# Scaled probabilities, split convolution scaling, and turned quarters on TensorE in a hybrid decoder layer

## Chip, cores and metric

One core of a Trainium2 chip runs the whole layer in one launch. The metric is device time in microseconds (us) of that launch, the median of several runs. A profiled execution stands beside them.

## What is computed

One layer of a hybrid decoder on 1024 tokens of width 1024, all in float32:

```python
h = rms_norm(x); P = h @ W_in + b_in            # [b_gate | c_gate | u | q | k | v]
conv = b_gate * conv3_causal(c_gate * u)        # 512 channels
p = exp(scores + bias - m)                      # window 128, two key blocks of 128 per query block
attn = (p / (sum(p) + exp(sink - m))) @ v       # 8 q heads, 2 kv heads, width 64
x = x + concat(rms_norm(conv), rms_norm(attn)) @ W_out + b_out
h2 = rms_norm(x); top-4 of 32 experts, gates = softmax of the four logits
y[e] = (min(g, 7) * sigmoid(1.702 * min(g, 7)) * (clip(l, -7, 7) + 1)) @ w2[e] + b2[e]
       # hid = h2 @ w1[e] + b1[e], g = even columns, l = odd columns
out = x + sum over the chosen experts of gate * y[e]
```

## The kernel before

Synchronisation is written by hand: each engine has its own instruction stream, and semaphores (`event`) tie them. The order within an engine is the order of the text. SP issues the weight loads, GpSimd (POOL) the indirect gathers and scatters.

**The mixer** (function `mixer`) goes over 8 blocks of 128 tokens, block 0 and block 7 written out, the others in a loop. In a block TensorE projects the four convolution chunks (`project_conv`, line 839), turns q and k (895), makes the scores (906), then turns the probabilities (`turn_p`, 850): for each half i of four heads and each key block j, four products of a 128x128 square of `probs` with a diagonal matrix `diag`, whose diagonal is 1/denominator, so that the product is the scaled transpose. `attend` (862) multiplies with v; it waits for the pT copies of both halves, of which DVE makes (i,0) (`read_turned`, 668) and ScalarE (i,1) (`turn_read_act`, 513). Then come the convolution part of the output projection (923, two halves of four k), with the sum of the convolution's squares between the halves (869), the first transposes of the next block's rows (804), the attention part (936), the next block's q projection (813), the transposes of h2 (945), k and v (817), the router (829, 954). DVE's order in a block is: gate_input (615), taps (622 to 627), gate_output (634) of the chunks, bias and maximum of the scores (645, 709, 716), `normalise` of each half (660 to 662), the copies (668), sums of squares (729, 737), the rest. GpSimd does the taps of chunks 2 and 3 (`add_taps_pool`, 439 to 445), then scales all of conv_y to conv_s in one instruction (462), the reciprocal roots (429), and adds b_out to the residual (468).

**The join.** The second function, `experts`, starts behind a barrier. DVE splits the gates into three bfloat16 parts (1341 to 1345), makes `token`, `limits` and `marks`, reads each token's rank in its expert from TensorE (1354), and works out a table of jobs, sorted by size (1358 to 1399). From it come the list of the first job's tokens (`match_tokens`, `list_tokens`, `read_list`) and two gathers of their rows on GpSimd (1213). ScalarE copies some counters and clears the banks (1266 to 1271). TensorE turns the biases (1674, 1677), which DVE copies (1444 to 1446). `first_rows` turns the gathered rows (1582, 16 squares; each of four steps needs both gathers), and DVE copies them to xT (1407).

**The jobs.** A job is one expert with up to 256 tokens: here 15 wide jobs (over 128 tokens, lines 1601, 1412 to 1438) and 17 narrow ones (up to 128). Each loads six slots of 2 MB of weights. A slot is loaded again for the next job once TensorE has used it (SP, 1157). In a narrow job (`narrow_job`) the token rows are the stationary side: `first_layer` has 4 parts of 512 columns (1625), `second_layer` 2 outputs of 512 columns over 8 k (1637), in the order m=0 and m=1 over k 0 to 5, then m=0 and m=1 over k 6 and 7. Each part of the first layer goes through DVE (`clip_rows`, `finish_rows`), ScalarE (sigmoid, 1298) and DVE again (`turn_act`, 16 transposes of 32x64, 1138) into act_T, of which part c holds k = 2c and 2c+1. Then DVE turns the next job's gathered rows into xT (`turn_x`, 16 transposes of 32x256, 1138), scales b2 by the gates (1543), and forms the output rows (1548), which GpSimd adds to the output (1257). The gather for the next job (1213) is issued after its list is read, behind part 1. TensorE's next job waits for xT.

Of the kernel before, what the change touches and what calls it, by code (L numbers as in the profile page):

```python
# [23 lines left out]
P = 128  # L24
# [111 lines left out]
def mixer(nc, x_rows, out_rows, h2_rows, rel_rows, norm_mix, w_in, b_in, conv_w, q_norm, k_norm, sinks,  # L136
          rel_bias, out_norm_conv, out_norm_attn, w_out, b_out, norm_ffn, w_router, b_router, const,
          cst, tri_b, ones_b, picked, gates, before):

    ident = cst[:, C_ID:C_ID + P]  # L140
    with ExitStack() as ctx:
# [65 lines left out]
        diag = sb("diag", [P, NH, P])  # L207
# [84 lines left out]
        conv_scaled = event("conv_scaled")  # L292
        conv_summed = event("conv_summed")
# [8 lines left out]
        diag_ready = [event(f"diag_ready_{i}") for i in ("first", "second")]  # L302
# [28 lines left out]
        vstep = Steps(sem("vector_step"), 23)  # L331
# [84 lines left out]
        def _(pool):  # L416
# [30 lines left out]
            def one_block(t, more, first=False):  # L447
# [32 lines left out]
        def _(act):  # L480
# [40 lines left out]
            def one_block(t, more):  # L521
# [13 lines left out]
                exp_half(t, 1)  # L535
                add_u_bias(t, 3)
# [32 lines left out]
        def _(dve):  # L569
# [86 lines left out]
            def normalise(t, i):  # L656
# [36 lines left out]
            nc.vector.tensor_copy(ones_b[:], cst[:, C_ONES:C_ONES + P])  # L693
            def one_block(t, more, first=False):
# [106 lines left out]
        def _(pe):  # L801
# [42 lines left out]
            def turn_p(t, i):  # L844

                wait(pe, diag_ready[i], t)
# [41 lines left out]
            def one_block(t, more):  # L888
# [73 lines left out]
def experts(nc, h2_rows, out_rows, w1, b1, w2, b2, cst, tri_b, ones_b, picked, gates, before):  # L962
# [8 lines left out]
    with ExitStack() as ctx:  # L971
# [338 lines left out]
        def _(dve):  # L1310
# [139 lines left out]
            for i in range(4):  # L1450
                read_xT(0, i)
# [305 lines left out]
```

## Time and profile before

| | |
|---|---|
| median of 3 runs | 2076.33 us (2073.55 to 2079.98) |
| profiled execution | 2082.2 us |
| its span, first to last instruction | 2080.4 us |
| mean granted TensorE clock | 0.979 |
| busy: PE, DVE, ACT, POOL | 1982.3, 1418.9, 352.5, 238.6 us |
| moved by DMA | 504.21 MB, mean 242 GB/s |

Engines: PE is TensorE's matmuls, PEld its weight loads, which overlap them, DVE VectorE, ACT ScalarE, POOL GpSimd, SP SyncE. A row of the timeline has its start, its length (of one instruction, or of a group of neighbours with their count), the engine, the line and what it writes and reads; the bracket tells idle time ahead of it and what ended it. A float32 matmul shows as two instructions (passes), a transpose by the identity as one. A PE instruction's length reaches past the start of the next, since matmuls are pipelined.

### The profile page before, as it was taken

The numbers are of one execution on the slowest core, as the hardware profiler recorded it, in microseconds if no ns is written. First come the engines' busy times: TensorE is split into PE (matmuls) and PEld (weight loads), VectorE is DVE, ScalarE is ACT, GpSimd is POOL, SyncE is SP. The second block draws the span as 40 slices with busy tenths as digits, with TensorE's granted clock in tenths as the row PEclk, the third lists the DMA queues.
The fourth block names the chain that finished last, engine by engine and source line by source line (L and its number), as shares of the span: only waits on it lengthen the run. The fifth ranks groups of instructions, "written<-read, shape, count | busy, mean of one in ns | idle before, by whom it ended". The sixth has DMA issues, their size and how long they took to land.

```text
span 2080.4 us, 30074 instructions
## 1 busy us (share of the span) xinstructions
PE 1982.3 (95%) x10692; PEld 1453.0 (70%) x10692; DVE 1418.9 (68%) x4145; ACT 352.5 (17%) x732; POOL 238.6 (11%) x305
## 2 busy tenths in 40 slices
PE   7899999994999999989999999999999999999996
PEld 6577777772999999989999999834444444444442
DVE  3345545544276677777876777778887888788876
ACT  2122222221011222212222222210000000000000
POOL 1212222211000111110011111110000000000000
PEclk9999999996899999999999999999999999999998
DMA  9411001002956777767788888999999999999992
GB/s 299 102 41 40 20 30 40 30 31 94 334 169 232 233 259 247 271 211 263 266 283 282 301 294 294 324 332 327 366 356 355 368 367 359 358 362 368 367 353 67
DMA packets 238481, 504.21 MB, mean 242 GB/s; under 512 B 7525, under 2 KB 20881, under 8 KB 236257
## 3 DMA queue, kind: packets, MB, share of 16 engines
q1 hardware_dynamic: 224736, 454.93, 61.1%
q0 software_dynamic: 11392, 40.18, 7.8%
q10 hardware_dynamic: 2304, 8.39, 1.0%
q8 instruction: 38, 0.62, 0.1%
q14 instruction: 11, 0.08, 0.0%
HBM read 475.48 MB, written 28.00 MB: 242 GB/s over the span
## 4 chain that ended last, share of the span: by engine, by line
issue 41%; PE 28%; POOL 2%; DMA 2%; DVE 2%; POOLq 0%; ACT 0%; DVEq 0%
PE ps_unit L1601 28%; DMA out_dram<-y_rows,idx_cur 1%; POOL out_dram L1257 1%; POOL x_got L1213 1%; DMA x_got<-h_rows,idx_next 0%; DVE act_T L1422 0%; DVE sig L1420 0%; DVE glu L1412 0%; ACT sig L1280 0%; PE ps_list L1570 0%; PE ps_unit L1582 0%; POOL carrier L1209 0%; POOL out_dram L1225 0%; POOLq L990 0%; DVE match L1325 0%
## 5 line engine op out<-in xcount | busy, mean ns | idle before, releaser
L1601 PE MATMUL ps_unit<-xT,w_slot 128*128 128x136 f32 (+6 forms) x3840 | 528.3, 300 | 16.3 <-issue 15.3
L1601 PEld LDWEIGHTS ps_unit<-xT,w_slot 128*128 128x128 f32 x3840 | 523.0, 198 | 17.6 <-issue 17.5
L1625 PE MATMUL ps_unit<-w_slot,xT 128*128 128x512 f32 x1088 | 477.2, 597 | 8.1 <-DVE xT L1138 8.1
L1625 PEld LDWEIGHTS ps_unit<-w_slot,xT 128*128 128x128 f32 x1088 | 204.5, 190 | 266.3 <-issue 266.3
L1138 DVE STREAM_TRANSPOSE xT<-x_got 32x256 f32<-32x256 f32 x668 | 291.1, 436 | 16.9 <-DMA x_got<-h_rows,idx_next 7.7
L1601 PE MATMUL ps_unit<-act_T,w_slot 128*128 128x136 f32 (+6 forms) x1920 | 264.0, 299 | 7.0 <-DVE act_T L1422 6.7
L1138 DVE STREAM_TRANSPOSE act_T<-act_rows 32x64 f32<-32x64 f32 x1088 | 256.8, 236 | 16.3
L1601 PEld LDWEIGHTS ps_unit<-act_T,w_slot 128*128 128x128 f32 x1920 | 259.5, 191 | 10.0 <-DVE act_T L1422 5.6
L1637 PE MATMUL ps_unit<-w_slot,act_T 128*128 128x512 f32 x544 | 236.5, 592 | 1.3 <-DVE act_T L1138 1.3
L1438 DVE STREAM_TRANSPOSE y_rows<-yT 32x256 f32<-32x256 f32 x396 | 172.6, 436 | 38.9 <-ACT yT L1287 33.5
L1637 PEld LDWEIGHTS ps_unit<-w_slot,act_T 128*128 128x128 f32 x544 | 103.3, 190 | 131.7 <-issue 129.4
L839 PE MATMUL ps_c<-hT,w_in_sb 128*128 128x128 f32 x1536 | 176.8, 276 | 0.0
L839 PEld LDWEIGHTS ps_c<-hT,w_in_sb 128*128 128x128 f32 x1536 | 173.5, 192 | 3.1 <-issue 3.1
L1209 POOL TENSOR_TENSOR carrier<-carrier 128x1 f32<-128x1 f32 x64 | 15.0, 235 | 1393.0 <-issue 592.5
L1298 ACT ACTIVATE sig<-glu 128x256 f32<-128x256 f32 x68 | 28.3, 416 | 646.1 <-DVE glu L1504 646.1
L1412 DVE TENSOR_SCALAR glu<-ps_unit,b_cur 128x256 f32<-128x256 f32 x120 | 57.5, 480 | 77.5 <-PE ps_unit L1601 76.9
L1420 DVE TENSOR_TENSOR sig<-sig,glu 128x256 f32<-128x256 f32 x120 | 51.0, 425 | 69.6 <-ACT sig L1280 52.6
L1280 ACT ACTIVATE sig<-glu 128x256 f32<-128x256 f32 x120 | 50.0, 417 | 276.7 <-DVE glu L1412 276.5
L1500 DVE TENSOR_TENSOR hid<-ps_unit,b_row 128x512 f32<-128x512 f32 x68 | 47.0, 691 | 72.5 <-PE ps_unit L1625 72.4
L1287 ACT ACTIVATE yT<-ps_unit,b_cur 128x256 f32<-128x256 f32 x120 | 50.4, 471 | 210.2 <-PE ps_unit L1601 210.2
L923 PE MATMUL ps_s<-w_out_sb,conv_s 128*128 128x512 f32 x128 | 61.0, 622 | 6.9 <-DMA w_out_sb<-in_w_out_dram 6.9
L1292 ACT ACTIVATE y_rows<-y_rows,gate_cur 128x1024 f32<-128x1024 f32 x30 | 32.8, 1141 | 179.2 <-DVE y_rows L1438 179.2
(247 smaller groups left out, 1505.9 us busy)
## 6 DMA issues: line engine op xcount, KB each, us to landing
w_slot<-in_w_dram SPq DMA_DIRECT2D x192, 2048.0 KB, 10.4
b_row<-in_b_dram SPq DMA_DIRECT2D x17, 1024.0 KB, 12.1
b_row<-in_b_dram SPq DMA_DIRECT2D x17, 512.0 KB, 13.6
w_in_sb<-in_w_in_dram SPq DMA_DIRECT2D x12, 512.0 KB, 8.5
x_in<-in_x_dram SPq DMA_DIRECT2D x8, 512.0 KB, 3.5
x_res<-in_x_dram SPq DMA_DIRECT2D x8, 512.0 KB, 4.9
out_dram<-x ACTq DMA_DIRECT2D x8, 512.0 KB, 5.1
h_rows<-h ACTq DMA_DIRECT2D x8, 512.0 KB, 3.2
```

The source lines that it names most:

```text
L839: last = pe.matmul(ps_c[:, c % 2, j * P:(j + 1) * P], w_in_sb[:, k, first:first + P], hT[:, k, :], start=(k == 0), stop=(k == KD - 1))
L923: last = pe.matmul(ps_s[:, n * 512:(n + 1) * 512], conv_s[:, k, :], w_out_sb[:, k, n * 512:(n + 1) * 512], start=(k == 0), stop=(k == CC - 1))
L1138: last = nc.vector.transpose(out[c * Q:(c + 1) * Q, :, tokens], rows.rearrange("p (k c j) -> p k c j", c=P // Q, j=Q)[:, :, c, :])
L1280: nc.scalar.activation(sig[:, p % 3, :], glu[:, p % 3, :], ACT.Sigmoid, scale=ALPHA).then_inc(sig_ready[p].sem, 1)
L1287: last = nc.scalar.activation(yT[:, m, :], ps_unit[p % RING][:, u, :], ACT.Identity, bias=b2_cur[:, m:m + 1])
L1412: v.tensor_scalar(glu[:, p % 3, :], ps_unit[p % RING][:, 0, :], b1_cur[:, 2 * p:2 * p + 1], LIMIT, ALU.add, ALU.min).then_inc(glu_ready[p] ...
L1420: v.tensor_tensor(sig[:, p % 3, :], sig[:, p % 3, :], glu[:, p % 3, :], ALU.mult).then_inc(scaled[p].sem, 1)
L1438: last = v.transpose(rows[:, :, c, :], yT[c * Q:(c + 1) * Q, :, a * Q:(a + 1) * Q])
L1500: v.tensor_tensor(hid[:, c % 2, :], ps_hid[c], b1_row[:, c * LW:(c + 1) * LW], ALU.add).then_inc(hid_read[c].sem, 1)
L1601: last = pe.matmul(ps_unit[p % RING][:, u, 0:n], w, moving[:, k, 0:n], start=(k == 0), stop=(k == KD - 1))
L1625: last = pe.matmul(ps_hid[c], xT[:, k, 0:P], w_slot[:, c, k, :], start=(k == 0), stop=(k == KD - 1))
L1637: last = pe.matmul(ps_out[m], act_T[:, k, 0:P], w_slot[:, W1_LOADS + m, k, :], start=(k == 0), stop=(k == KD - 1))
```

## The change

- Probabilities: `diag` and its product are gone. DVE multiplies the first half of `probs` by 1/denominator; the second half is scaled by four ScalarE instructions after its exponentials. TensorE turns `probs` with the identity.
- conv_s is scaled in two instructions on GpSimd: chunks 0 to 2 ahead of the taps of chunk 3, and chunk 3 after them. TensorE waits for the second at k = 3 of the first half.
- `token`, `limits`, `marks` are made by DVE in the mixer, ahead of block 0.
- In the join ScalarE does the three casts of the gates, the reads of the turned biases and two of the four xT copies. DVE's second subtraction moves behind the job fields. `first_rows` turns all first halves after the first gather, then all second halves.
- Narrow jobs: the last part of act_rows (k = 6, 7) is turned by TensorE, two transposes between m=0 and m=1 over k 0 to 5, into a bank of its own, and copied by ScalarE. ScalarE also scales b2.

```diff
 # mixer, GpSimd
-                add_taps_pool(t, 3)
-                for i in range(CC):
+                for i in range(CC - 1):
                     wait(pool, conv_out[i], t)
                 wait(pool, conv_mixed, t - 1)
-                nc.gpsimd.tensor_tensor(conv_s[:], conv_y[:], conv_g_col.unsqueeze(2).broadcast_to([P, CC, P]),
+                nc.gpsimd.tensor_tensor(conv_s[:, 0:3, :], conv_y[:, 0:3, :], conv_g_col[:, 0:3].unsqueeze(2).broadcast_to([P, 3, P]),
                                         ALU.mult).then_inc(conv_scaled.sem, 1)
+                add_taps_pool(t, 3)
+                wait(pool, conv_out[3], t)
+                nc.gpsimd.tensor_tensor(conv_s[:, 3:4, :], conv_y[:, 3:4, :], conv_g_col[:, 3:4].unsqueeze(2).broadcast_to([P, 1, P]),
+                                        ALU.mult).then_inc(conv_scaled_last.sem, 1)
 # mixer, ScalarE
                 exp_half(t, 1)
+                wait(act, denom_ready, t)
+                for s in range(HALF, NH):
+                    last = nc.scalar.activation(probs[:, s, :], probs[:, s, :], ACT.Copy, scale=rdenom[:, s:s + 1])
+                last.then_inc(probs_ready[1].sem, 1)
                 add_u_bias(t, 3)
 # mixer, VectorE, normalise
+                if i == 1:
+                    nc.vector.reciprocal(rdenom[:, part], denom[:, part]).then_inc(denom_ready.sem, 1)
+                    return
                 then_wait(t, nc.vector.reciprocal(rdenom[:, part], denom[:, part]))
-                nc.vector.tensor_tensor(diag[:, part, :], ident.unsqueeze(1).broadcast_to([P, HALF, P]),
-                                        rdenom[:, part].unsqueeze(2).broadcast_to([P, HALF, P]),
-                                        ALU.mult).then_inc(diag_ready[i].sem, 1)
+                nc.vector.tensor_tensor(probs[:, part, :], probs[:, part, :],
+                                        rdenom[:, part].unsqueeze(2).broadcast_to([P, HALF, 2 * P]),
+                                        ALU.mult).then_inc(probs_ready[i].sem, 1)
 # mixer, TensorE
-                        last = pe.matmul(ps_turned[i][j][:, h * P:(h + 1) * P], probs[:, s, j * P:(j + 1) * P], diag[:, s, :],
-                                         start=True, stop=True)
+                        last = pe.transpose(ps_turned[i][j][:, h * P:(h + 1) * P], probs[:, s, j * P:(j + 1) * P], ident)
...
+                        if n == 0 and k == CC - 1:
+                            wait(pe, conv_scaled_last, t)
 # experts, ScalarE
+            nc.scalar.copy(gate_parts[:, :, 0, :], gates[:]).then_inc(parts_cast[0], 1)
...
+            act.wait_ge(biases_turned, 1)
...
+            for i in (0, 2):
+                wait(act, x_turned[i], 0)
+                nc.scalar.copy(xT[:, 2 * i:2 * i + 2, :], ps_x[i][:]).then_inc(xT_read, 1)
...
+                wait(act, last_turned, t)
+                nc.scalar.copy(act_T[:, KD - 2:KD, 0:P], ps_act[:, 0:2, :]).then_inc(actT_ready[W1_LOADS - 1].sem, 1)
+                wait(act, b2_loaded, t)
+                wait(act, cur_ready, q)
+                nc.scalar.activation(b2_row[:], b2_row[:], ACT.Copy, scale=gate_cur[:, 0:1]).then_inc(b2_gated.sem, 1)
 # experts, VectorE, narrow job
-                    turn_act(t, c)
+                    if c < W1_LOADS - 1:
+                        turn_act(t, c)
...
-                wait(dve, b2_loaded, t)
-                v.tensor_scalar(b2_row[:], b2_row[:], gate_cur[:, 0:1], None, ALU.mult).then_inc(b2_gated.sem, 1)
 # experts, TensorE
+            def turn_last(t):
+                wait(pe, rows_ready[W1_LOADS - 1], t)
+                first = (W1_LOADS - 1) % 2 * PW
+                for k in range(2):
+                    last = pe.transpose(ps_act[:, k, :], act_rows[:, first + k * P:first + (k + 1) * P], ident)
+                last.then_inc(last_turned.sem, 1)
...
-                for ks in (range(0, 6), range(6, KD)):
-                    for m in range(2):
-                        second_layer(t, q, m, ks)
+                second_layer(t, q, 0, range(0, KD - 2))
+                turn_last(t)
+                second_layer(t, q, 1, range(0, KD - 2))
+                for m in range(2):
+                    second_layer(t, q, m, range(KD - 2, KD))
...
-                for i in range(4):
-                    turn_x(0, i)
+                for h, gathered in enumerate((gathered_a, gathered_b)):
+                    wait(pe, gathered, 0)
+                    for i in range(4):
+                        turn_x(i, h)
```

## Rows read from the trace of the kernel before

**Rows 1.** Busy time by stretches: us, busy us by engine, PEclk, DMA share, GB/s

```profile
271.00:324.00 53.00, 53.00 (x324) 38.51 (x323) 25.84 (x62) 14.53 (x39) 11.07 (x16) 1.00 0.12 40
1498.00:1540.00 42.00, 41.69 (x105) 18.36 (x104) 34.54 (x119) 2.95 (x5) 3.02 (x4) 1.00 1.01 363
1389.00:1392.50 3.50, 3.50 (x5) 1.32 (x4) 3.19 (x13) 0.00 (x0) 1.68 (x2) 0.53 1.04 392
```

**Rows 2.** Who waited for whom, whole run: us in total, times, longest

```profile
PE ps_unit L1625 <- DVE xT L1138: 8.1, 16, 3.4
...
PE ps_s L923 <- DMA w_out_sb<-in_w_out_dram: 6.9, 1, 6.9
```

**Rows 3.** Timeline of one block of the mixer, TensorE (start us, us, what)

```profile
234.88 1.06 PE L850 MATMUL ps_q<-diag,probs 128*128 128x128 f32 x8
...
238.60 1.94 PE L862 MATMUL ps_c<-pT,v_keys 128*64 128x512 f32 x8
...
262.44 1.04 PE L945 MATMUL ps_s<-cst,h 128*128 128x128 f32 x8
263.31 2.32 PE L817 MATMUL ps_kv<-w_in_sb,hT 128*128 128x256 f32 x10
```

**Rows 4.** The same block, VectorE

```profile
230.67 0.69 DVE L662 TENSOR_TENSOR diag<-cst,small 128x512 f32<-128x512 f32 x1
...
237.76 0.69 DVE L668 COPY pT<-ps_s 128x512 f32<-128x512 f32 x1 [1.09 <-PE ps_s L850]
```

**Rows 5.** The same block, ScalarE

```profile
231.88 0.49 ACT L506 ACTIVATE probs<-probs,small 128x256 f32<-128x256 f32 x1
...
235.08 0.37 ACT L498 ACTIVATE conv_u<-ps_c,vectors 128x128 f32<-128x128 f32 x1 [2.52 <-PE ps_c L839]
```

**Rows 6.** The same block, GpSimd

```profile
231.70 1.11 POOL L439 TENSOR_TENSOR conv_t<-conv_x,vectors 128x128 f32<-128x128 f32 x3 [16.29 <-DVE conv_x L615]
...
238.97 1.04 POOL L462 TENSOR_TENSOR conv_s<-conv_y,vectors 128x512 f32<-128x512 f32 x1 [0.80 <-DVE conv_y L634]
```

**Rows 7.** Timeline of the join between mixer and experts

```profile
496.85 0.17 DVE L1339 SCALAR_TENSOR_TENSOR token<-cst 128x8 f32<-128x8 f32 x1 [1.34 <-PEq L126]
...
499.37 0.42 DVE L1354 COPY rank<-ps_list 128x256 f32<-128x256 f32 x1
...
510.50 0.16 DVE L1332 COPY list_sb<-ps_list 128x10 f32<-128x10 f32 x1
...
523.17 3.65 PE L1582 MATMUL ps_unit<-cst,x_got 128*128 128x128 f32 x16 [12.94 <-DMA x_got<-h_rows,idx_next]
...
527.88 4.45 PE L1601 MATMUL ps_unit<-xT,w_slot 128*128 128x208 f32 x12 [1.06 <-DVE xT L1407]
```

**Rows 8.** The tile x_got from 505 to 530 us: two gathers, issue to landing

```profile
DMA to landing us min/median/max: 7.8/8.8/9.9
```

**Rows 9.** Timeline of the narrow jobs in their steady state

```profile
1460.29 13.90 PE L1637 MATMUL ps_unit<-w_slot,act_T 128*128 128x512 f32 x32
...
1462.98 3.98 DVE L1138 STREAM_TRANSPOSE act_T<-act_rows 32x64 f32<-32x64 f32 x16
...
1466.99 7.18 DVE L1138 STREAM_TRANSPOSE xT<-x_got 32x256 f32<-32x256 f32 x16
...
1474.50 14.00 PE L1625 MATMUL ps_unit<-w_slot,xT 128*128 128x512 f32 x32 [0.31 <-DVE xT L1138]
...
1496.07 1.01 POOL L1213 DMA_INDIRECT x_got<-h_rows,idx_next  x1
...
1516.56 3.69 PE L1625 MATMUL ps_unit<-w_slot,xT 128*128 128x512 f32 x8 [0.31 <-DVE xT L1138]
```

**Rows 10.** DMA issues of the page: count, KB each, median us to landing

```profile
w_slot<-in_w_dram SPq DMA_DIRECT2D x192, 2048.0 KB, 10.4
...
x_got<-h_rows,idx_next POOLq DMA_INDIRECT x49, 7.0
```

**Rows 11.** Timeline, start of the second narrow job

```profile
1388.68 15.69 PE L1625 MATMUL ps_unit<-w_slot,xT 128*128 128x512 f32 x32 [3.41 <-DVE xT L1138]
```

More of the change, by code:

```diff
@@ L137, in mixer @@
           rel_bias, out_norm_conv, out_norm_attn, w_out, b_out, norm_ffn, w_router, b_router, const,
-          cst, tri_b, ones_b, picked, gates, before):
+          cst, tri_b, ones_b, picked, gates, before, token, limits, marks):
     ident = cst[:, C_ID:C_ID + P]
@@ L206, in mixer @@
         pT = sb("pT", [P, 2, 2, HALF * P])
-        diag = sb("diag", [P, NH, P])
         attn_ss = sb("attn_ss", [P, P])
@@ L301, in mixer @@
         exped = [event(f"exped_{i}") for i in ("first", "second")]
-        diag_ready = [event(f"diag_ready_{i}") for i in ("first", "second")]
+        denom_ready = event("denom_ready_second")
+        probs_ready = [event(f"probs_ready_{i}") for i in ("first", "second")]
         p_turned = [[event(f"p_turned_{i}{j}") for j in range(2)] for i in ("first", "second")]
@@ L693, in _ @@
             nc.vector.tensor_copy(ones_b[:], cst[:, C_ONES:C_ONES + P])
+            nc.vector.scalar_tensor_tensor(out=token[:], in0=cst[:, C_TOK:C_TOK + NB], scalar=32.0,
+                                           in1=cst[:, C_TOK + NB:C_TOK + 2 * NB], op0=ALU.mult, op1=ALU.add)
+            nc.vector.tensor_scalar(limits[:, 0, :], cst[:, C_IOTA:C_IOTA + len(SIZES) - 1], float(SIZE_STEP), float(SIZES[0]),
+                                    ALU.mult, ALU.add)
+            nc.vector.tensor_scalar(marks[:], cst[:, C_IOTA:C_IOTA + len(SIZES)], float(P),
+                                    float(P * (2 - len(SIZES))), ALU.mult, ALU.add)
             def one_block(t, more, first=False):
@@ L844, in turn_p @@
             def turn_p(t, i):
-                wait(pe, diag_ready[i], t)
+                wait(pe, probs_ready[i], t)
                 for j in range(2):
@@ L959, in _, with experts @@
             one_block(NB - 1, False)
-def experts(nc, h2_rows, out_rows, w1, b1, w2, b2, cst, tri_b, ones_b, picked, gates, before):
+def experts(nc, h2_rows, out_rows, w1, b1, w2, b2, cst, tri_b, ones_b, picked, gates, before, token, limits, marks):
     ident = cst[:, C_ID:C_ID + P]
@@ L1008, in experts @@
         place_cur = sb("place_cur", [P, NB])
-        token = sb("token", [P, NB])
         match = sb("match", [P, NB, CAP], BF16)
@@ L1049, in experts @@
         ps_list = ps("ps_list", [P, 512])
+        ps_act = ps("ps_act", [P, 4, P])
         ps_x = ps_unit[2:]
@@ L1070, in experts @@
         rstep = Steps(sem("routing_step"), 0)
+        parts_cast = [sem(f"gate_part_cast{i}") for i in range(3)]
+        parts_left = [sem(f"gate_part_left{i}") for i in range(2)]
         units_cleared = sem("units_cleared")
@@ L1265, in _ @@
         def _(act):
+            nc.scalar.copy(gate_parts[:, :, 0, :], gates[:]).then_inc(parts_cast[0], 1)
             nc.scalar.copy(iota_b[:], cst[:, C_IOTA:C_IOTA + CAP]).then_inc(counters_copied, 1)
+            act.wait_ge(parts_left[0], 1)
+            nc.scalar.copy(gate_parts[:, :, 1, :], other[:]).then_inc(parts_cast[1], 1)
             nc.scalar.copy(entry[:, :, 0], cst[:, C_TOK:C_TOK + NB]).then_inc(counters_copied, 1)
@@ L1402, in _ @@
             dve.wait_ge(counters_copied, 3)
+            dve.wait_ge(parts_cast[2], 1)
             dve.wait_ge(table_ready, TABLES)
             match_tokens(0, bass.ds(first_expert, 1), base_row[:, 0:1])
-            def read_xT(t, i):
-                wait(dve, x_turned[i], t)
-                v.tensor_copy(xT[:, 2 * i:2 * i + 2, :], ps_x[i][:]).then_inc(xT_read if i < 3 else xT_ready.sem, 1)
             def clip(q, p):
@@ L1572, in list_tokens, with turn_x @@
                 last.then_inc(listed.sem, 1)
-            def turn_x(t, i):
-                if i == 0:
-                    wait(pe, gathered_a, t)
-                    wait(pe, gathered_b, t)
+            def turn_x(i, h):
                 for c in range(2):
-                    for h in range(2):
-                        k = 2 * i + c
-                        last = pe.transpose(ps_x[i][:, c, h * P:(h + 1) * P], x_got[:, h, k * P:(k + 1) * P], ident)
-                last.then_inc(x_turned[i].sem, 1)
+                    k = 2 * i + c
+                    last = pe.transpose(ps_x[i][:, c, h * P:(h + 1) * P], x_got[:, h, k * P:(k + 1) * P], ident)
+                if h == 1:
+                    last.then_inc(x_turned[i].sem, 1)
             def piece(q, p, n):
```

52 lines of the change are left out of this document (27 added, 25 removed).

## Prediction

> **What bounds the kernel now.** I read the busy time by stretches first, then the waits, then the timeline of one piece of each stage. The first [rows 1] tells the stages apart. In the mixer's loop TensorE is busy for all 53 us of a 53 us stretch at full clock while the DMA share is 0.12: TensorE binds, and an instruction less on it counts in full unless something else comes last. In the join between the two halves of the program (some 490 to 528 us) TensorE stands still for 12.94 us before the first token rows arrive [rows 7]: a chain through several engines and a gather binds there. In the narrow jobs TensorE is busy 41.69 of 42 us, but the DMA share is 1.01 too. The waits [rows 2] say which of the two ends last: in the narrow jobs TensorE waited for the turned token rows (DVE, line 1138) 16 times, 8.1 us together with 3.4 the longest; no wait of TensorE there is put down to a weight load. One more wait matters: 6.9 us in the first block, for the load of w_out.
>
> **Part 1: probabilities turned with the identity.** The matmul with `diag` takes two passes; a block has 32 instructions of them, 8 for each group of 4 heads. They start at 234.88 and the next kind, held 0.15 by a copy, at 238.60 [rows 3], so they take (238.60-0.15-234.88)/32 = 0.112 us each, 3.58 us in all. A transpose is one pass: the 8 of line 945 start at 262.44 and the next instruction at 263.31, 0.109 us each. Sixteen take 1.75 us, so TensorE is offered 1.8 us a block. It can't take all: `attend` (line 862, started at 238.60) needs pT of both halves. Count from C = 234.88, the end of the last convolution projection. ScalarE's conv_u(3) starts at 235.08 and takes 0.37 [rows 5]; DVE's `gate_input(3)` waits for it, from about 235.55, and takes about as long, so DVE is free at C+1.02. It copies pT(0,0) in 0.62 to 0.69 and pT(1,0) in as much (line 668 [rows 4]), done at C+2.36; TensorE followed the same copy by 0.15 before (237.76+0.69 [rows 4] to 238.60 [rows 3]), so `attend` starts at C+2.51 = 237.39. The gain is 1.21 us a block, and 0.6 us of new idle time stands on TensorE in front of `attend`. Bounds: 0, if another link is late, and 1.8.
>
> Is something late? DVE's product for the first half was 512 elements in 0.69 us from 230.67 [rows 4]; with 1024 it is about 1.3, 0.6 more. It is needed at 234.9 and ready at 231.9. It moves `gate_input(2)` and with it GpSimd's taps of chunk 2 by 0.6, from 231.70 to 232.3 [rows 6]; they and the conv_y after them end near 235.25, and `gate_input(3)` could not start before 235.55 anyway. The second half goes to ScalarE: four copies with a scale on 256 elements. Their nearest row is the exponential of the same tile, 0.49 us with its accumulator [rows 5]; at 0.4 to 0.5 each, from 233.2, they end at 234.8 to 235.2, up to 0.1 into conv_u(3), and 0.6 before TensorE wants them (C+0.9). I take no cost, at worst 0.1 a block.
>
> **Part 2: conv_s in two instructions.** GpSimd now scales three chunks (of 1.04 us for four [rows 6], some 0.8) ahead of the taps of chunk 3. Those wait for `gated[3]` at 235.9 and then start at 236.25 where they started at 235.98; conv_out[3] comes at 238.85, 0.15 later. Behind it stand ScalarE's squares, DVE's conv_ss at about 241.8, and TensorE's sum after the first half of the convolution mix, now at 237.4 + 1.9 for `attend` [rows 3] + 3.4 for 8 passes of 512 columns (0.43 each, [rows 9]) = 242.7. One us to spare. The last chunk is scaled by 239.4 and wanted at 241.9. Without this split `attend` would end at 239.25 and the mix would wait for conv_s until 240.0, so the edit keeps 0.8 of the 1.21 but adds nothing of its own.
>
> Mixer: the first block stands still behind w_out's load (6.9 us [rows 2], larger than any gain ahead of it), seven blocks x 1.21 = 8.5 us. The three small DVE instructions moved in ahead of block 0 (0.5 us) lie behind that wait.
>
> **Part 3: the join.** DVE took 499.37 - 496.85 = 2.52 us [rows 7] from its first instruction to the copy of rank. With three instructions moved out and the casts on ScalarE, there stays the wait for one cast and one subtraction, at 0.42 each by the rank copy of the same size: 0.85, so 1.67 saved. The second subtraction comes back later ahead of `other` (0.45): 1.2 net, for the job table and the weight loads. The three bias copies, over 1.0 us in front of the first list on DVE (it starts at 510.50), go to ScalarE, but the list comes only 0.3 before they end: 1.5 us saved up to the gather. The gathers landed 7.8 and 9.9 us after their issues [rows 8], the second issued after the first. Then TensorE turned 16 squares in 3.65 us from 523.17 (0.228 each, half clock), and the first weights were used at 527.88 [rows 7]: 4.7 us from landing to start. Now eight are done while the second gather is under way (1.8 us; it lands over 2.1 later), eight remain, and the last copy of 0.69 follows with two waits: 1.8+0.3+0.7+0.3 = 3.1. Saved 1.6. Part 3: 1.5+1.6 = 3.1 us; ends 1 (the gathers, which share the DMA with the first weights, land no earlier) and 5 (the clock rises earlier too).
>
> **Part 4: narrow jobs.** A job lasts 1516.56 - 1474.50 = 42.06 us [rows 9]. The second layer starts at 1460.29 and its 32 passes take 0.429 each, up to 1474.0; the next job's first pass starts at 1474.50, behind DVE's transposes of the token rows (from 1466.99, 7.18 us), and its weights couldn't be loaded early. The stall is 0.31 us by the waits and about 0.5 by the passes. DVE now leaves out the last 16 squares (3.98 us from 1462.98) and the scaling of b2: it starts on the token rows at 1462.95 and ends at 1470.2, 4 us early. The gather they wait for is issued 21.57 us into the job before (1496.07 against 1474.50), so at 1454.0 for this one, and lands 7.0 later at the median [rows 9, 10]: 1461. The stall goes. TensorE gets two transposes instead. Bounds: 0.22 (two pitches of 0.109) and 0.6 (each exposing a weight load of its own and of its neighbour); I take 0.25, since the four-, six- and eight-transpose groups of the mixer run at their pitch between other matmuls. rows_ready comes at 1462.95, TensorE turns it after six k at 1465.4; ScalarE copies by 1466.5 and k=6 is wanted at 1470.8. ScalarE's scaling of b2 (about 1.2 us) ends at 1468, wanted at 1472.6. Net 0.31 us x 15 jobs = 4.65.
>
> What is late next is the DMA: it has to move the same bytes in 41.75 us. A weight load lands 10.4 us after its issue at the median [rows 10], and a slot that comes free is wanted again 35 us later (42 less the 7 of its own use); that cover is gone only if landings triple. I charge nothing.
>
> The first narrow job is worse off before: its successor starts 3.41 us late and takes 15.69 instead of 14.0 us for 32 passes [rows 9, 11], and the granted clock from 1389 to 1392.5 is 0.53, near the lower of its two levels (1.2 against 2.4 GHz), where it is 1.00 in the other stretches [rows 1]. DVE's 4.7 us less ends the 3.41; the new transposes wait 0.75 for their rows and cost 0.25: 2.6 saved, with 1.7 more if the clock then holds. I count 4.3. In the last job the two y_rows instructions, at 0.7 each like DVE's other reads of 512 elements (0.69 [rows 4]), started behind the token rows and b2, about 1475.0 in this job's time, and ended at 1476.4. Now the first runs under the end of the second layer (1474.3), the second ends at 1475.2: some 1.1 us saved. Part 4: 4.65+4.3+1.1 = 10.1; ends 0 (the stall only changes its cause) and 14 (15 x 0.56 and the two others).
>
> A rule speaks against parts 1 and 4. The Trainium skill, "TensorE: Matmul & The Clock Gate", Part 4, gives about 275 ns for a transpose in a kernel's context and says that transposes don't count as work for the clock. The rows of line 945 agree on the duration (the last of the eight ends 0.28 us after it starts [rows 3]) and not on the pitch of neighbours, 0.109 at full clock; by the page's figure, if it were the pitch, an estimate of part 1 is a loss of 0.8 us a block and of part 4 nothing.
>
> **Sum.** 8.5+3.1+10.1 = 21.7 us. The profiled execution took 2082.2 us (span 2080.4), 5.9 above the median of 2076.33, so it would be 2060.5 and the median 2054.6. A measurement here can tell some 0.3%, 6 us, from no change.
>
> **The rivals.** (a) *The narrow period stays*, because two transposes expose their loads (0.56 and not 0.25), or because the DMA share of 1.01 is the real limit. For it: that share. Against it: no wait for a weight. It takes back 4.65: 2059.3. Chance 0.17.
> (b) *The mixer gives nothing*: the 0.6 us that DVE gets in the first half or the four copies on ScalarE arrive late at `attend`, so its start stays at 238.6. For it: my slack on ScalarE is 0.6. Against it: DVE's is 3 us. 2063.1. Chance 0.13.
> (c) *More than forecast*: `attend` takes the whole 1.8 (7 x 0.6 = 4.2 more) and one slow-clock stretch less falls in the wide jobs (1.7): 2049. Chance 0.08.
> (d) *Slower*: 16 transposes and the new gap ahead of `attend` bring the clock to half in every block. Price: a slow stretch of 3.5 us, as the one at 1389 [rows 1, 11], costs 1.7, and transposes one after the other at their whole duration (1.04 - 7 x 0.109 = 0.28 [rows 3]) cost 0.8 over the old matmuls: 2.5 x 8 = 20, less parts 3 and 4 (13.2): 2083. It decides from 1.7 us a block. Against it: each block holds 22 transposes now and its clock is 1.00 [rows 1]. This is where the page's rule on the clock would lead; so far the trace speaks against it. Chance 0.04.
> (e) *The shorter stages come out elsewhere*: what the mixer and the join save is waited for again in the wide jobs, whose start only moves, and the narrow part gives half. 2071. Chance 0.04.
>
> **How the numbers follow.** The forecast has 0.54, with its own range 2050 to 2060. Down to 2048 and up to 2067 takes in (a), (b) and most of (c). Faster by over 0.3% (below 2070.1): forecast, (a), (b), (c), less a little for runs that scatter by 6 us: 0.91. Within: (e), 0.05. Slower: (d), 0.04.
>
> **What would show it.** In the changed profile: `turn_p` with 128 instructions in eight blocks and not 256, at a pitch near 0.11; `attend` 2.5 us after the last projection; a block period 1.2 us shorter; the first expert weights used 11.6 us earlier, 8.5 of it from the mixer; a narrow period of 41.75 with no wait for the turned token rows; the half-clock stretch near 1389 gone. The forecast is wrong if `attend` or the mix waits for ScalarE or GpSimd, if the narrow period stays 42.0, or if a clock below 1 appears inside the mixer's loop.

## The result and the profile after

| | before | after |
|---|---|---|
| median of 3 runs | 2076.33 us | 2053.82 us (2052.48 to 2058.19) |
| profiled execution | 2082.2 us | 2052.48 us |
| its span | 2080.4 us | 2050.7 us |
| mean granted TensorE clock | 0.979 | 0.982 |
| busy: PE, DVE, ACT | 1982.3, 1418.9, 352.5 us | 1964.6, 1337.1, 394.4 us |

The ratio after to before is 0.9887, 95% interval 0.9864 to 0.991: 22.5 us less between the medians, where 21.7 was forecast (2054.6). The profiled executions lie 29.7 apart, because the one of before was 5.9 above its median and the one of after 1.3 below. That difference splits by marks of TensorE in the two traces as follows; what stands in the last column was the forecast of the same piece.

| from, to | before | after | less | forecast |
|---|---|---|---|---|
| start to block 0's output projection | 67.04 | 64.00 | 3.04 | 0 |
| to its first instruction behind the barrier | 429.81 | 420.18 | 9.63 | 8.5 |
| join, to the first expert weights | 31.03 | 27.45 | 3.58 | 3.1 |
| wide jobs | 814.19 | 811.64 | 2.55 | 0 |
| first narrow job | 46.61 | 43.99 | 2.62 | 2.6 |
| from there to the end of the span | 691.72 | 683.44 | 8.28 | 7.5 |

Busy time by stretches of the changed kernel (us, then busy us of PE, PEld, DVE, ACT and POOL, PEclk, DMA share, GB/s), answering to [rows 1]:

```profile
271.00:324.00 53.00, 52.54 (x318) 37.96 (x317) 25.90 (x59) 15.61 (x41) 11.39 (x17) 1.00 0.11 40
1468.00:1510.00 42.00, 42.00 (x108) 18.76 (x107) 30.36 (x103) 4.37 (x7) 3.02 (x4) 1.00 1.01 364
```

The mixer's loop has its clock at 1.00 with the transposes in it, and TensorE is now idle for 0.46 us of 53. In a narrow stretch DVE is busy 30.36 us instead of 34.54, TensorE all 42, and the DMA share is still 1.01.

The same block of the mixer as [rows 3], TensorE:

```profile
226.75 2.40 PE L856 MATMUL ps_c<-hT,w_in_sb 128*128 128x128 f32 x20
228.98 0.60 PE L867 MATMUL ps_q<-cst,probs 128*128 128x128 f32 x4
229.42 0.60 PE L867 MATMUL ps_kv<-cst,probs 128*128 128x128 f32 x4
229.85 1.04 PE L867 MATMUL ps_s<-cst,probs 128*128 128x128 f32 x8
231.34 1.94 PE L878 MATMUL ps_c<-pT,v_keys 128*64 128x512 f32 x8 [0.45 <-DVE pT L679]
233.21 3.70 PE L941 MATMUL ps_s<-w_out_sb,conv_s 128*128 128x512 f32 x8
```

C, the end of the last convolution projection, is 228.98 here. The sixteen transposes follow each other at 0.109 us (0.44 for four), and `attend` starts at C+2.36, held 0.45 by DVE's copy. It started at C+3.72 [rows 3]. DVE and ScalarE of that block, answering to [rows 4, 5]:

```profile
229.65 0.35 DVE L623 SCALAR_TENSOR_TENSOR conv_x<-ps_c,vectors,conv_u 128x128 f32<-128x128 f32 x1 [0.75 <-ACT conv_u L502]
229.92 0.68 DVE L679 COPY pT<-ps_q 128x512 f32<-128x512 f32 x1
230.52 0.68 DVE L679 COPY pT<-ps_s 128x512 f32<-128x512 f32 x1
```

```profile
227.36 1.71 ACT L542 ACTIVATE probs<-probs,small 128x256 f32<-128x256 f32 x4 [0.69 <-DVE small L670]
229.18 0.37 ACT L502 ACTIVATE conv_u<-ps_c,vectors 128x128 f32<-128x128 f32 x1
```

The two copies on DVE run one after the other, and the second ends 0.14 us before `attend`. ScalarE's four scalings end at 229.07, before conv_u(3) wants the engine. GpSimd, answering to [rows 6]:

```profile
229.13 0.83 POOL L462 TENSOR_TENSOR conv_s<-conv_y,vectors 128x384 f32<-128x384 f32 x1 [0.62 <-DVE conv_y L642]
230.08 1.12 POOL L440 TENSOR_TENSOR conv_t<-conv_x,vectors 128x128 f32<-128x128 f32 x3
...
232.73 0.40 POOL L466 TENSOR_TENSOR conv_s<-conv_y,vectors 128x128 f32<-128x128 f32 x1 [0.46 <-DVE conv_y L642]
```

The last chunk is ready at 233.13, before the mix starts (233.21). In the kernel before the mix of this block started here:

```profile
240.46 3.70 PE L923 MATMUL ps_s<-w_out_sb,conv_s 128*128 128x512 f32 x8
```

The join, answering to [rows 7]; the five lines of DVE in the middle stand here for a reason that comes below:

```profile
484.18 0.37 PE L1717 MATMUL ps_list<-picked,tri_b 128*128 128x256 bf16 x1 [4.43 <-PEq L126]
...
488.17 1.80 POOL L1210 MEMSET x_got<- 128x2048 f32 x1
488.20 0.16 DVE L1407 SCALAR_TENSOR_TENSOR order_key<-size,past 128x1 f32<-128x1 f32 x1
488.39 1.61 DVE L1409 TENSOR_SCALAR reached<-marks,order_key 128x12 bf16<-128x12 f32 x1
488.53 1.47 DVE L1411 TENSOR_SCALAR fields<-ended 128x1 bf16<-128x1 f32 x1
488.60 1.41 DVE L1412 CAST fields<-size 128x1 bf16<-128x1 f32 x1
488.66 1.35 DVE L1413 CAST fields<-first 128x1 bf16<-128x1 f32 x1
488.72 1.29 DVE L1415 TENSOR_TENSOR gates<-other,gate_parts 128x256 f32<-128x256 f32 x1
490.06 0.79 PE L1723 MATMUL ps_list<-cst,order_key 128*128 128x128 f32 x2 [5.27 <-DVE reached L1409]
...
498.56 1.05 POOL L1232 DMA_INDIRECT x_got<-h_rows,idx_next  x1 [8.58 <-DVE idx_next L1374]
499.91 0.96 POOL L1232 DMA_INDIRECT x_got<-h_rows,idx_next  x1 [0.31 <-issue]
...
506.48 3.82 PE L1605 MATMUL ps_unit<-cst,x_got 128*128 128x128 f32 x16 [9.25 <-DMA x_got<-h_rows,idx_next]
...
511.63 4.61 PE L1625 MATMUL ps_unit<-xT,w_slot 128*128 128x208 f32 x15 [1.32 <-DVE xT L1479]
```

The two gathers from issue to landing, answering to [rows 8], and, below, the second gather of the kernel before in the chain that ended last (start us, us):

```profile
DMA to landing us min/median/max: 7.8/8.1/8.4
```

```profile
513.13 9.91 DMA x_got<-h_rows,idx_next
```

The second gather landed 8.4 us after its issue here and 9.9 before.

The narrow jobs, TensorE, answering to [rows 9] (steady state, second layer from 1436.73) and, in the first lines, to [rows 11] (end of the first narrow job and start of the second):

```profile
1358.40 0.44 PE L1671 MATMUL ps_act<-cst,act_rows 128*128 128x128 f32 x2 [0.50 <-DVE act_rows L1543]
1358.68 8.75 PE L1661 MATMUL ps_unit<-w_slot,act_T 128*128 128x512 f32 x20
1367.26 13.90 PE L1649 MATMUL ps_unit<-w_slot,xT 128*128 128x512 f32 x32
...
1408.97 13.90 PE L1649 MATMUL ps_unit<-w_slot,xT 128*128 128x512 f32 x32
...
1436.73 5.31 PE L1661 MATMUL ps_unit<-w_slot,act_T 128*128 128x512 f32 x12
1441.88 0.38 PE L1671 MATMUL ps_act<-cst,act_rows 128*128 128x128 f32 x2
1442.10 8.75 PE L1661 MATMUL ps_unit<-w_slot,act_T 128*128 128x512 f32 x20
1450.68 4.88 PE L1649 MATMUL ps_unit<-w_slot,xT 128*128 128x512 f32 x11
```

The period is 1450.68 - 1408.97 = 41.71 us (42.06 before), with no idle time between the jobs; the two transposes take 1442.10 - 1441.88 = 0.22. The second job's first 32 passes take 13.90 and not 15.69 us: the half-clock stretch that followed the 3.41 us wait [rows 11] is gone, as is all but 0.50 us of the wait, which now stands ahead of the first job's two transposes.

### The profile page after: what moved, and what is told of

The parts are those of the page before. It is cut to its first block, busy times and chain, and to the rows that moved or that the text cites. A ratio compares the mean times of both kernels' runs of the same rounds, so it can differ in the third digit from the quotient of the medians.

```text
span 2050.7 us, 29692 instructions
## 1 busy us (share of the span) xinstructions
PE 1964.6 (96%) x10598; PEld 1439.9 (70%) x10598; DVE 1337.1 (65%) x3840; ACT 394.4 (19%) x806; POOL 237.3 (12%) x313
## 4 chain that ended last, share of the span: by engine, by line
issue 39%; PE 32%; DVE 1%; DMA 1%; POOL 1%; ACT 0%; POOLq 0%; DVEq 0%
PE ps_unit L1625 32%; DMA out_dram<-y_rows,idx_cur 1%; POOL x_got L1232 1%; DMA x_got<-h_rows,idx_next 0%; PE ps_list L1597 0%; DVE act_T L1454 0%; DVE sig L1452 0%; DVE glu L1444 0%; ACT sig L1315 0%; PE ps_unit L1605 0%; POOL carrier L1228 0%; POOL out_dram L1276 0%; POOL out_dram L1244 0%; DVE match L1365 0%; DVE reached L1409 0%
## 5 line engine op out<-in xcount | busy, mean ns | idle before, releaser
L1157 DVE STREAM_TRANSPOSE act_T<-act_rows 32x64 f32<-32x64 f32 x816 | 192.6, 236 | 12.2
```

What stands on the lines that cost most here:

```text
L1157: last = nc.vector.transpose(out[c * Q:(c + 1) * Q, :, tokens], rows.rearrange("p (k c j) -> p k c j", c=P // Q, j=Q)[:, :, c, :])
```

## The experiments

The theory was the prediction's own: about 9 us from the mixer, 3 from the join, 10 from the narrow jobs, each from the place named there. Its rivals were that the split of conv_s does nothing, that a transpose costs more than its pitch, that the DMA sets the narrow period, and that the 3.0 us of the first row of the table belong to the change.

**Each part alone.** The first four kernels of this section share the runs of the kernel before (median 2079.54 us). The first has the change in `mixer` alone, less the three instructions moved into it:

```diff
 # against the kernel before: mixer
-last = pe.matmul(ps_turned[i][j][...], probs[...], diag[:, s, :], start=True, stop=True)
+last = pe.transpose(ps_turned[i][j][...], probs[...], ident)
 # and the scaling of probs on DVE and ScalarE, and conv_s in two instructions
```

> The mixer's edits alone (identity transposes, ScalarE's scaling, conv_s in two), join and jobs as before. Theory: each of blocks 1 to 7 is 1.36 us shorter, 9.5 us in all, and the whole is 9.5 us faster (ratio 0.9954); the 3.0 us by which block 0's w_out load came earlier in the changed kernel's profile is scatter of that load and shows here or not by chance. Rival: that load comes earlier because of the change (fewer stores and reads beside it), so the first output projection starts near 64 us here too, and the gain is 12.5 us (ratio 0.994).

Measured: 2067.04 us, ratio 0.9937 (0.992 to 0.9953). From block 0's output projection to the barrier the trace shows 421.07 us, 8.7 less than before; the first eight passes of that projection took 6.54 us here and 5.81 before, and behind them 9.5 are saved, as expected. That projection started at 64.70 us. It did so at 64.77 and 65.70 in the next two kernels, whose mixer turns the probabilities as before, and at 67.38 in a second trace of the changed kernel: the 3.0 us are scatter of the load of w_out [rows 2]. The medians alone don't say so: they are 12.5 us apart, the rival's number, and the theory's 0.9954 lies just outside the interval. Of these 12.5 the trace places 8.7 in the mixer; the other 3.8 are not placed.

The second has the join alone:

```diff
 # against the kernel before: experts, up to the first rows; token, limits, marks in mixer
+nc.scalar.copy(gate_parts[:, :, 0, :], gates[:])     # the casts, on ScalarE
+for h, gathered in enumerate((gathered_a, gathered_b)):
+    wait(pe, gathered, 0)                             # first rows by halves
```

> The join's edits alone (casts, bias reads and two xT copies on ScalarE, three instructions moved ahead, first rows by halves). Theory: from the first instruction behind the barrier to the first expert weights 27.5 us instead of 31.0, so 3.5 us faster in all (ratio 0.9983), and block 0's output projection starts near 67 us as before. Rival: the weights' load sets the first use, and the join gives under 1 us. The wide jobs should keep their length of 814 us; if they come out 2.5 us shorter as in the changed kernel, that part hangs on the later code and not on scatter.

Measured: 2077.45 us over 10 runs, ratio 0.9991 (0.9978 to 1.0003). The join took 27.60 us in the trace, as in the kernel with everything (27.45). Of 3.4 us a median shows 2.1 and an interval that reaches to nothing. Part of the difference is the trace of before: the unchanged join took 31.03 us there, but 29.76 with the mixer alone and 30.56 with the narrow jobs alone, mostly because the second gather landed 9.9, 8.9 and 9.5 us after its issue. Beside those two traces the saving is 2.2 to 3.0 us; a saving of 0.1 to 0.2% is at the edge of what such runs can tell, and here the trace says more than the time.

The third has the narrow jobs alone:

```diff
 # against the kernel before: experts, narrow jobs
-for ks in (range(0, 6), range(6, KD)):
-    for m in range(2):
-        second_layer(t, q, m, ks)
+second_layer(t, q, 0, range(0, KD - 2))
+turn_last(t)
+second_layer(t, q, 1, range(0, KD - 2))
+for m in range(2):
+    second_layer(t, q, m, range(KD - 2, KD))
 # and the copy to act_T and the scaling of b2 on ScalarE
```

> The narrow jobs' edits alone. Theory: period 41.71 us instead of 42.06 (15 times 0.35), first narrow job 2.6 shorter, no half clock behind it (1.7), last job 1.2 shorter: 10.8 us faster in all (ratio 0.9948). Rival: the DMA, with a share of 1.01, sets the period; then it would stay at 42.0 and the gain be some 5.5 us (ratio 0.9973).

Measured: 2069.28 us, ratio 0.9949 (0.9931 to 0.9967). The period is 41.71 us again, and the second narrow job starts at full clock. The three ratios leave out 0.0063, 0.0009 and 0.0051, together 0.0123, where the whole change leaves out 0.0113: within their intervals the parts add up, and none needs another.

**conv_s in one instruction again**, the rest of the change kept:

```diff
-for i in range(CC - 1):
+add_taps_pool(t, 3)
+for i in range(CC):
     wait(pool, conv_out[i], t)
-nc.gpsimd.tensor_tensor(conv_s[:, 0:3, :], ...)
-add_taps_pool(t, 3)
-wait(pool, conv_out[3], t)
-nc.gpsimd.tensor_tensor(conv_s[:, 3:4, :], ...)
+nc.gpsimd.tensor_tensor(conv_s[:], ...)
```

> The changed kernel with conv_s scaled in one instruction again, after the taps of chunk 3. Theory: conv_y of chunk 3 is ready 3.7 us after the last projection, the scaling ends 1.1 to 1.2 later, near C+4.9, where the output projection could start at C+4.23: 0.7 us of wait in each of seven blocks, 4.9 us slower than the changed kernel (ratio to before 0.9915). Rival: the order on GpSimd is what made conv_y of chunk 3 late (the taps wait behind the scaling), so without the split it comes 0.4 earlier and the loss is only 0.3 a block, 2 us (ratio 0.9899).

Measured: 2061.87 us, ratio 0.9912 (0.9895 to 0.9928); from block 0's output projection to the barrier 425.75 us, 5.6 more than with the split. The interval holds both the theory's ratio and the rival's; the trace decides between them. TensorE and GpSimd of the same block:

```profile
235.22 1.94 PE L875 MATMUL ps_c<-pT,v_keys 128*64 128x512 f32 x8 [0.45 <-DVE pT L676]
237.88 3.70 PE L936 MATMUL ps_s<-w_out_sb,conv_s 128*128 128x512 f32 x8 [0.73 <-POOL conv_s L463]
```

```profile
236.79 1.04 POOL L463 TENSOR_TENSOR conv_s<-conv_y,vectors 128x512 f32<-128x512 f32 x1 [0.64 <-DVE conv_y L639]
```

The mix waits 0.73 us for the whole of conv_s in each of 7 blocks. That is the wait which the prediction's part 2 expected without the split (0.8 a block): the edit is worth more than half of part 1 together with it. By itself it should be worth nothing, since in the trace of before conv_s ends at 240.01 [rows 6] and the mix starts at 240.46; it was not run alone.

**Four transposes in place of two** in each narrow job (each square turned twice):

```diff
-for k in range(2):
+for k in (0, 1, 0, 1):
     last = pe.transpose(ps_act[:, k, :], ...)
```

> The changed kernel with each of the two transposes of a narrow job's last part done twice (four instead of two), nothing else. Theory: a transpose costs TensorE its pitch and hides its weight load, 0.11 us each; the narrow period goes from 41.71 to 41.93. Rival: transposes cost their whole length of about 0.28 one after the other, then 42.25.

Measured: one run of 2056.43 us. TensorE in the steady state:

```profile
1409.48 13.90 PE L1649 MATMUL ps_unit<-w_slot,xT 128*128 128x512 f32 x32
...
1442.38 0.60 PE L1671 MATMUL ps_act<-cst,act_rows 128*128 128x128 f32 x4
1442.82 8.75 PE L1661 MATMUL ps_unit<-w_slot,act_T 128*128 128x512 f32 x20
1451.41 4.03 PE L1649 MATMUL ps_unit<-w_slot,xT 128*128 128x512 f32 x9
```

The period is 41.93, 0.22 more for two transposes more: 0.11 each, the pitch and not their length, although matmuls stand on both sides.

**Less to load.** Biases b1 and b2 of the narrow jobs are brought to 8 partitions instead of 128, and the two tiles are cleared at the start, so that most tokens of these jobs get no bias:

```diff
-sp.dma_start(b1_row[:], src.partition_broadcast(P))
+sp.dma_start(b1_row[0:8, :], src.partition_broadcast(8))
...
-sp.dma_start(b2_row[:], src.partition_broadcast(P))
+sp.dma_start(b2_row[0:8, :], src.partition_broadcast(8))
 # and the memsets of b1_row and b2_row on GpSimd, for which SP waits
```

> The changed kernel with the narrow jobs' b1 and b2 loaded into 8 partitions instead of 128 (1.4 MB less of some 15 MB a job; the other rows use zeros, so it leaves out part of the biases, and clears those tiles first). Theory: the DMA is not what sets the narrow period; its share falls from 1.01 to about 0.92 and the period stays 41.71. Rival: the DMA sets it, and it falls by up to a tenth.

Measured: one run of 2053.23 us. The same stretch as in the changed kernel's second row above:

```profile
1468.00:1510.00 42.00, 42.00 (x108) 18.75 (x107) 30.34 (x104) 4.37 (x7) 3.02 (x4) 1.00 0.94 328
```

The DMA share falls from 1.01 to 0.94 and the period stays at 41.71. The DMA doesn't set it: a share of 1.01 here is no proof of a bound.

**The memset moved.** The join came out near its forecast, but with something new in it: the five DVE instructions above start one by one from 488.39 and all end near 490.0, where GpSimd's memset of x_got ends (488.17 + 1.80 = 489.97). TensorE waits for the first of them. Here the memset goes behind the event after which the list of jobs is made:

```diff
-nc.gpsimd.memset(x_got[:], 0.0).then_inc(buffers, 1)
 pool.wait_ge(carrier_cleared, 1)
+pool.wait_ge(order_ready, 1)
+nc.gpsimd.memset(x_got[:], 0.0).then_inc(buffers, 1)
```

> The changed kernel with GpSimd's clearing of x_got moved behind the order of the jobs (order_ready). In the changed kernel five VectorE instructions that start at 488.39 to 488.72 all end at 489.97 to 490.0, together with that clearing (488.17 to 489.97). Theory: the first of them, a tensor_scalar that writes bfloat16, cannot run beside the clearing; with the clearing later they take 0.15 to 0.4 each again, and the join (barrier to first weights, 27.45 us) is 1.2 to 1.4 us shorter. Rival: they waited for something else, and nothing changes; or the clearing meets other such instructions and the wait only moves.

Measured: one run of 2052.21 us; DVE, TensorE and GpSimd at that place:

```profile
488.71 0.23 DVE L1410 TENSOR_SCALAR reached<-marks,order_key 128x12 bf16<-128x12 f32 x1
488.85 0.15 DVE L1412 TENSOR_SCALAR fields<-ended 128x1 bf16<-128x1 f32 x1
...
489.00 0.80 PE L1724 MATMUL ps_list<-cst,order_key 128*128 128x128 f32 x2 [3.90 <-DVE reached L1410]
...
491.34 1.80 POOL L1212 MEMSET x_got<- 128x2048 f32 x1 [2.79 <-DVE order L1426]
```

The first instruction takes 0.23 instead of 1.61 us, TensorE's wait falls from 5.27 to 3.90, the first gather is issued 13.40 instead of 14.38 us after the barrier, and the join falls from 27.45 to 26.40 us. The memset held them.

**The copies by halves.** `attend` waits for DVE, which makes two copies in a row of squares that TensorE has turned first and third. With the turning ordered by key block, DVE copies both blocks of the first half and ScalarE both of the second:

```diff
-for i in range(2):
-    turn_p(t, i)
+for j in range(2):
+    for i in range(2):
+        turn_p(t, i, j)
 # DVE
-read_turned(t, 1, 0)
+read_turned(t, 0, 1)
 # ScalarE
-turn_read_act(t, 0)
-turn_read_act(t, 1)
+for j in range(2):
+    turn_read_act(t, 1, j)
```

> The changed kernel with VectorE copying both pT parts of the first half and ScalarE both of the second, and TensorE turning in the order (0,0), (1,0), (0,1), (1,1). Theory: attend waits only because VectorE copies two parts one after the other; now it starts at C+1.85 instead of C+2.36, 0.5 us less in each of seven blocks, 3.5 us in all (ratio to before 0.987). Rival: ScalarE's probabilities of the second half, wanted 0.9 earlier, come late (they end at C+0.1 to C+0.3, wanted at C+0.44), or the sum of the convolution's squares becomes the wait, and nothing is won.

Measured: 2054.43 us (2053.29 to 2054.67), ratio 0.9886 (0.987 to 0.9903). TensorE of the block:

```profile
229.41 0.60 PE L867 MATMUL ps_q<-cst,probs 128*128 128x128 f32 x4
...
230.72 0.60 PE L867 MATMUL ps_s<-cst,probs 128*128 128x128 f32 x4
231.29 1.94 PE L878 MATMUL ps_c<-pT,v_keys 128*64 128x512 f32 x8
```

`attend` starts at C+1.88 with no wait put down to DVE, and from block 0's output projection to the barrier it is 417.61 us instead of 420.18: 2.6 of the 3.5 expected. The blocks themselves are 0.49 us shorter each; the first eight passes of that projection took 6.49 us in this trace and 5.66 in the changed kernel's. The time doesn't show it: beside the changed kernel's 0.9887 the ratio is 0.0001 lower, where 0.0017 was expected. In the profiled run TensorE stood still for 1.47 us more for the second gather in the join, and the wide jobs took 814.15 us, 2.5 more than in the changed kernel's trace. That left open whether the gain is real or is lost downstream each time, so both edits were run together, beside the changed kernel itself, on the same chip and against the same runs of before:

> The changed kernel with both of the last two edits: the copies of the turned probabilities by halves, and the memset of x_got behind order_ready. Theory (the edits are independent and both lie on the path): mixer from block 0's output projection to the barrier at 417.6 us as in the run with the copies by halves, join at 26.4 us where both gathers land in time, so 3.5 us less than the changed kernel: 2050 to 2051 us beside 2054 in the same call, ratio to the kernel before 0.0017 lower than that of the changed kernel. Rival (the halves of the copies only shift the wait to another place behind the profile's own scatter, and the join waits for its second gather anyway): within 1 us of the changed kernel in the same call.

> The changed kernel itself once more, in the same call as the version with both edits, so that the two share the runs of the kernel before. Theory: 2054 us, ratio to the kernel before 0.989, 3.5 us above the version with both edits. Rival: within 1 us of it.

Measured: both edits 2050.34 us (4 runs, 2047.27 to 2052.57), ratio 0.9861 (0.9843 to 0.9879); the changed kernel 2056.48 us (5 runs, 2054.79 to 2059.36), ratio 0.989 (0.9875 to 0.9905), beside 2078.46 for the kernel before. The ratio is 0.0029 lower, where 0.0017 was expected, and the rival, within 1 us of each other, falls. Every run of the first is below every run of the second, though the two intervals overlap at their ends (0.9875 to 0.9879). Between the two traces the mixer from block 0's output projection is 417.20 against 420.61 us, the join 26.45 against 27.71, the wide jobs 808.8 against 811.5, and the first narrow job (43.99) and the period (41.71) are equal. So 4.7 us are where the theory put them, 3.4 in the mixer and 1.3 in the join. The wide jobs' 2.7 and 1.0 at the load of w_out are of the size by which these pieces differ between kernels that don't differ there. The kernel with both edits is the fastest of this study.

## Why the prediction was right

**The forecast held, in the mixer and the narrow jobs for its reasons, in the join partly by luck.** The median came 0.8 us below the forecast. The step that didn't hold is in part 3, "1.5 us saved up to the gather": 0.54 was, and a gather that landed 1.5 us sooner than in the trace of before, which nothing in the prediction foresaw, made up for it. The other terms were right or a little small, and two pieces that were counted at nothing moved by themselves.

*Part 1, the mixer.* The step "`attend` starts at C+2.51" was mis-sized by 0.15: it starts at C+2.36. The rows taken from before gave DVE's first copy at C+1.02 and two copies of 0.62 to 0.69; it starts at C+0.94 and the second follows after 0.60. A block saves 1.36, not 1.21, and 7 x 1.36 = 9.5 of the 9.63 measured. That the saved time is not the 1.8 us which the transposes free, and that DVE is what ends last, was as predicted. The estimate for DVE's product (1.3 us) measured 1.22, and ScalarE's four scalings, put at 0.4 to 0.5 each, 0.43. They end 0.78 us before TensorE turns the second half at 229.85, which is the slack that rival (b) doubted (0.6 in the prediction).

*Part 2, the split.* As predicted, 0.73 a block measured for 0.8. The taps of chunk 3 were forecast 0.27 us later than before and start at C+1.10 as before: the three chunks are scaled by 229.96, just ahead of them.

*Part 3, the join.* 3.58 for 3.1, and not in the pieces of the forecast. From the barrier to the issue of the first gather 14.38 us instead of 14.92, so 0.54 saved for 1.5. From the landing of the second gather to the first weights 3.32 instead of 4.85, so 1.53 saved for 1.6. The rest, 1.5, is the second gather itself, 8.4 us from issue to landing instead of 9.9. It is scatter at least in part: with the old join it took 8.9 to 9.9 in three traces, with the new one 8.4 to 8.7 in eight and 10.0 in one, the copies by halves, whose join was 28.99. With 9.9 the changed join would have taken some 1.5 us more and saved some 2.1.

What the first piece lacks is the memset: moved away, it gives back 0.98 at the gather (13.40 for 14.38), so that 1.52 are saved there, which is the forecast's 1.5. In the whole join it cost 1.05 us (27.45 against 26.40), or 1.26 with the copies by halves beside it (27.71 against 26.45). No row of before showed it. The prediction took work out of DVE's chain; that brought the bfloat16 outputs of DVE forward onto GpSimd's memset. In the trace of before the memset (500.85 to 502.65) ends 0.19 us ahead of the same instruction, so 0.2 us of gain on DVE were enough to meet it.

*Part 4, the narrow jobs.* 0.35 a job for 0.31. The stall that went was 0.57 (0.35 and the 0.22 of the two transposes); the prediction gave it as 0.31 by the waits and about 0.5 by the passes, and neither of these less its cost of 0.25 gives its net of 0.31; only the 0.56 of its upper end does. In the first job 2.62 for 2.6, but that number too doesn't follow from its terms, 3.41 - 0.75 - 0.25 = 2.41: the transposes waited 0.50 for their rows and took 0.28, and 3.41 - 0.50 - 0.28 = 2.63. Behind it 1.7 from the clock for 1.7 (the second job took 43.76 us before, 1.70 more than the jobs after it, and takes 41.71 like them now), and 1.3 in the last job for 1.1. Together 10.9 for 10.1.

*The rivals.* (a), the DMA as the limit, fell by the run with fewer bytes, and the exposed loads by the run with four transposes. (b) fell by the mixer alone, 0.9937. (d), a slower clock in the mixer, fell by the 1.00 of the loop. The Trainium skill, "TensorE: Matmul & The Clock Gate", Part 4, counts about 275 ns for a transpose and none of it as work for the clock. The duration agrees (the last of four ends 0.27 to 0.28 us after it starts), the pitch of 0.109 is what counts here, and the clock stayed at 1.00 with 38 transposes a block among matmuls; a kernel of transposes alone wasn't tried. (e) fell in the changed kernel's trace, where nothing saved ahead of the wide jobs came back in them. Of (c) one half came by itself: the wide jobs hold one slow-clock stretch less, below.

*What stays open.* The wide jobs took 811.6 us in the trace of the changed kernel, 814.2 in that of before, 816.7 with the mixer alone and 808.8 with both edits, all with the same instructions there. Most of that goes with TensorE's clock: each trace has two to four stretches at about 0.5 in the wide jobs, and the time lost in them, one minus the granted clock summed over windows of 2 us, is 8.6 us in the changed kernel, 12.4 before (3 stretches against 4), 13.7 with the mixer alone and 5.1 with both edits. TensorE's idle time there (21.0, 22.3, 22.1 and 21.0 us) differs less. What starts the stretches wasn't tried.

## What to carry to other kernels

When a faster step is followed by two consumers on two engines, count the copies between: the gain here was set by DVE's two copies and not by the transposes, and the next 0.5 us a block lay in which engine copies which half. A small edit such as the split of conv_s is worth what the large one would lose without it, so price it with the other in place. When an engine's work is taken forward, look at what the other engines do at the new place, and check a part of a forecast piece by piece even where its sum is right. And where a saving is below 0.2% of the time, look for it in the marks of the trace and confirm it with both kernels side by side, since pieces of this kernel that no edit touched differ by 4 us (the start of the first output projection, 63.5 to 67.4) and by 8 (the wide jobs, 808.8 to 816.7) between executions.

## What the runs showed that was not expected

**A GpSimd memset that held DVE.** The memset of x_got, 128x2048 float32, 1.80 us, held a DVE tensor_scalar of 12 elements a row with bfloat16 output for 1.61 us instead of 0.23, and as long (1.60 to 1.62) in the six other traces in which the two meet. The four instructions behind it ended with it. It did not hold everything: scalar_tensor_tensor of up to 32 elements a row and tensor_scalar of one, with float32 outputs, ran beside the same memset at 0.15 to 0.25 us in the trace of before (the memset from 500.85 to 502.65; the last row is the held instruction, there just behind it). Moved later (491.34 to 493.14), the memset also left two float32 tensor_tensor of 256 elements at 0.42 to 0.43 us.

```profile
501.15 0.25 DVE L1366 SCALAR_TENSOR_TENSOR junk_e<-last_job,cst,jobs_of 128x32 f32<-128x32 f32 x1
...
501.45 0.21 DVE L1368 TENSOR_SCALAR first<-started,cst 128x1 f32<-128x1 f32 x1
...
502.84 0.23 DVE L1378 TENSOR_SCALAR reached<-marks,order_key 128x12 bf16<-128x12 f32 x1
```

The Trainium skill, "SBUF — State Buffer", section "SBUF: two separate sides", says that DVE and GpSimd share a pair of ports, locked by one of them for a whole instruction when DVE runs in a two-port mode, and that the other then blocks. The held instruction, released at the memset's end, agrees with such a lock. Why DVE asks for it in that one was not tried: the held instruction differs from the tensor_scalar that ran freely in its output's type and in its 12 elements a row.

**Single transposes among matmuls cost their pitch.** Two, or four, between passes of 512 columns cost 0.11 us each, though each has a weight load of its own (the profile's page counts as many weight loads as matmuls, 10598 of each).
